# Product-key experts: four of eight token tiles gathered instead of two, keys swept in two passes and values in one

## The reference, cut to what matters

```python
q = (ht @ w_q).reshape(T, 8, 2, 128)
s = jnp.einsum('thpd,hpnd->thpn', q, sub_keys)          # 8 heads, 2 halves, 128 sub-keys
vals, idx = lax.top_k(s, 16)
cand = vals[:, :, 0, :, None] + vals[:, :, 1, None, :]   # 256 candidates a head
top_s, top_pos = lax.top_k(cand.reshape(T, 8, 256), 16)
experts = (i1 * 128 + i2)                                # 8 * 16 = 128 of 16384 experts a token
gates = jax.nn.softmax(top_s, axis=-1)
a = gelu(einsum('td,ted->te', xb, u_tab[eb]))            # key side
y = einsum('te,ted->td', gates * a, v_tab[eb])           # value side
x = x + gate2 * rmsnorm(y)
```

## Time and profile before

| | us |
|---|---|
| median of three runs | 3335.14 |
| lowest, highest | 3317.35, 3335.84 |
| profiled execution, first to last instruction | 3333.3 |
| PE, DVE, ACT, POOL busy | 3133.5, 2255.8, 1016.9, 1005.3 |
| first key product to last key product | 719.5 to 2218.6 |
| first value product to last value product | 2225.9 to 3307.5 |
| granted TensorE clock, mean | 0.976 |

### The profile page before, as it was taken

How to read it: one execution, slowest core, us unless ns; L and a number is a source line. 1 busy time by engine, 2 the same in 40 slices (tenths; PEclk the granted TensorE clock), 3 DMA queues, 4 the chain that set the end, 5 groups by cost and what they waited for, 6 DMA issues and landing times. The chain is left out here.

```text
span 3333.3 us, 44756 instructions
## 1 busy us (share of the span) xinstructions
PE 3133.5 (94%) x14706; PEld 2592.3 (78%) x14706; DVE 2255.8 (68%) x3986; ACT 1016.9 (31%) x1301; POOL 1005.3 (30%) x735
## 2 busy tenths in 40 slices
PE   3993799989999999999999999998999998999996
PEld 3881587878888888888888888876888886788885
DVE  6345643567767677675876754436888888888886
ACT  3123442112232232322222221122333334333333
POOL 0000100013222233232332310024555567765541
PEclk9995899999999999999999999999999999999998
DMA  6510122222333324333233332248999999999995
GB/s 235 189 50 8 49 105 93 84 72 113 126 148 139 148 88 151 141 149 137 101 142 145 150 137 106 102 159 299 373 353 361 364 357 332 369 357 364 348 361 186
DMA packets 251520, 640.90 MB, mean 192 GB/s; under 512 B 28864, under 2 KB 134464, under 8 KB 249792
## 3 DMA queue, kind: packets, MB, share of 16 engines
q1 hardware_dynamic: 204528, 498.87, 40.8%
q0 software_dynamic: 46928, 141.20, 11.3%
HBM read 505.76 MB, written 134.22 MB: 192 GB/s over the span
## 5 line engine op out<-in xcount | busy, mean ns | idle before, releaser
L1393 POOL TENSOR_TENSOR onehot<-onehot,slots 128x1024 fp32r<-128x1024 f32 x192 | 368.9, 1943 | 1180.1 <-DVE onehot L1479 1180.1
L93 PE MATMUL acc_u<-a_hi,u_hi 128*128 128x512 f32 x2048 | 633.1, 391 | 2.5 <-PEq L1114 2.5
L93 PE MATMUL acc_u<-a_lo,u_hi 128*128 128x512 f32 x2048 | 632.3, 390 | 0.0
L93 PE MATMUL acc_u<-a_hi,u_lo 128*128 128x512 f32 x2048 | 631.6, 389 | 0.0
L1882 PE MATMUL y_ps<-v_hi,c_hi 128*128 128x512 f32 x1536 | 477.2, 392 | 32.6 <-DVE c_lo L83 26.8
L1882 PE MATMUL y_ps<-v_lo,c_hi 128*128 128x512 f32 x1536 | 475.8, 391 | 0.0
L1882 PE MATMUL y_ps<-v_hi,c_lo 128*128 128x512 f32 x1536 | 474.6, 390 | 0.0
L78 ACT ACTIVATE v_hi<-v_raw 128x1024 fp32r<-128x1024 f32 x256 | 271.6, 1061 | 654.0 <-PE y_ps L1882 544.8
L93 PEld LDWEIGHTS acc_u<-a_lo,u_hi 128*128 128x128 f32 x2048 | 385.0, 188 | 81.0
L93 PEld LDWEIGHTS acc_u<-a_hi,u_lo 128*128 128x128 f32 x2048 | 384.8, 188 | 81.2
L83 DVE TENSOR_TENSOR v_lo<-v_raw,v_hi 128x1024 fp32r<-128x1024 f32 x256 | 316.6, 1237 | 186.4 <-ACT v_hi L78 145.1
(11 more groups left out here) (228 smaller groups left out, 3414.4 us busy)
## 6 DMA issues: line engine op xcount, KB each, us to landing
v_raw<-in_v SPq DMA_DIRECT2D x256, 512.0 KB
u_raw<-in_u SPq DMA_DIRECT2D x128, 512.0 KB, 4.3
act_d<-gelu SPq DMA_DIRECT2D x128, 512.0 KB, 2.6
gate_d<-gate_block SPq DMA_DIRECT2D x12, 4096.0 KB, 12.1
gt<-gate_d SPq DMA_DIRECT2D x64, 768.0 KB
at<-act_d SPq DMA_DIRECT2D x256, 192.0 KB
w_mod_b<-in_w_mod SPq DMA_DIRECT2D x6, 2560.0 KB, 9.1
w_mod<-in_w_mod SPq DMA_DIRECT2D x9, 1024.0 KB, 16.4
```

Of the source, the lines that this page charges most:

```text
L93: done = pe.matmul(acc[:, cols], w, a[:, k, cols], start=first, stop=last)
L1393: last_op = pool.tensor_tensor(onehot_2[u][:, :, part, :], onehot_2[u][:, :, 0, :].bitcast(F32), gate.unsqueeze(2).to_broadcast([P, TOK // ...
```

## The change

It touches everything after `mix_out`. One block `experts` takes the place of three; all loops are written out, and every engine's list runs over 384 steps m: 128 key blocks for the first three tiles (pass one), the same 128 key blocks for the other five (pass two), 128 value blocks for the last four tiles. The first four tiles are gathered. Three of them have their top-16 search in the retrieval stage, three tiles at a time; the other five have it in steps 5 to 204, two heads at a time. Gate tables of the four dense tiles are made in batches of 8 tokens, one batch in every third step from step 44. There GpSimd no longer computes: it only issues the 512 row and 512 activation fetches, which are consumed from step 134 on, two rows a step, three in steps 200 to 255. The candidate list of a head holds 136 sums instead of 256.

```diff
-SPARSE = 2
-DENSE = TT - SPARSE
+EARLY = 3
+GATHERED = 4
+LATE = TT - EARLY
+DENSE = TT - GATHERED
+HEAD_TILES = EARLY
+STAGES = 4
+RAWS, SPLITS, GELUS, ACTS, ROWS = 4, 3, 3, 4, 7
+TURN = 8
+STEP_STAGES = ((0, 1), (2,), (3,), (4, 5), (6, 7), (8, 9), (10,), (11,), (12,))
+TOPK_FROM, TOPK_PERIOD = 5, 40
+BATCH = 8
+GATE_BATCHES = P // BATCH
+GATE_STEPS = GATE_BATCHES + 1
+GATES_FROM, GATES_EVERY = 44, 3
+ROWS_FROM, ROWS_FAST = 134, 200
...
+def topk_stage(g, dve, stage, scores, tops_out, chosen_out, read_all, done):
...
+    dve.drain()
+    if stage == 0:
+        for c in cs:
+            for p in range(2):
+                dve.max(vals[:, c, p, 0:8], scores[c][p])
+    elif stage == 1:
+        for c in cs:
+            for p in range(2):
+                dve.max_index(idx[:, c, p, 1 - p:9 - p], vals[:, c, p, 0:8], scores[c][p])
+                last = dve.match_replace(rest[:, c, p, :], vals[:, c, p, 0:8], scores[c][p], LOWEST)
...
+def split_expert_hi(g, act, m):
+    act.wait_ge(g.raw_in[m % RAWS], 16 * (m // RAWS + 1))
+    if m >= SPLITS:
+        act.wait_ge(g.tile_done, m - SPLITS + 1)
+    split_hi(act, g.hi[m % SPLITS][:], g.raw[m % RAWS][:]).then_inc(g.hi_ready, 1)
...
+def expert_product(g, pe, m):
+    pe.wait_ge(g.lo_ready, m + 1)
...
+    if m < N:
+        parts = [(acc[:, 0:EARLY * P], slice(0, EARLY * P))]
+    else:
+        wide = LATE * P // 2
+        parts = [(acc[:, half * HALF:half * HALF + wide], slice(EARLY * P + half * wide, EARLY * P + (half + 1) * wide))
+                 for half in range(2)]
...
+def retrieval_scalar(g, act):
...
+    for n in range(QTILES):
+        act.wait_ge(g.q_done, n + 1)
+        act.activation(g.q[n % 2][:], g.mps[n % 2][:], ACT.Copy).then_inc(g.q_out, 1)
+        if n + 2 < QTILES:
...
+            split_hi(act, g.wq_hi[n % 2][:], g.wq_raw[n % 2][:]).then_inc(g.wq_hi_ready, 1)
...
+        if n:
+            stage_out(n - 1)
+def retrieval_vector(g, dve):
...
+    for h in range(HEADS - 1):
+        split(2 * h + 2)
+        dve.wait_ge(g.s_out, 2 * h + 2)
+        for stage in range(5):
+            head_stage(g, dve, h, stage)
+        split(2 * h + 3)
+        for stage in range(5, TOPK_STAGES):
...
+            head_stage(g, dve, h, stage)
+def retrieval_tensor(g, pe):
...
+    for n in range(2, QTILES):
+        score(n - 2)
+        product(n)
+    score(QTILES - 2)
+    expert_product(g, pe, 0)
+    score(QTILES - 1)
...
+def sweeps_scalar(g, act):
...
+    for m in range(3 * N):
+        if m >= 2 * N - 1 and m + 1 < 3 * N:
+            split_coefficients(m + 1 - 2 * N)
+        if m + 2 < 3 * N:
+            split_expert_hi(g, act, m + 2)
+        x, batch = gate_turn(m - 1)
+        if x is not None and batch >= 0:
+            gate_evacuation(x * GATE_BATCHES + batch)
...
+        if m < 2 * N:
+            activate(m)
...
+    def onehots(b, u):
...
+        for t in range(BATCH):
+            col = slice(first + t, first + t + 1)
+            dve.tensor_scalar(g.onehot_1[u][:, t, :], g.iota, g.slots[:, 0, col], None, ALU.is_equal)
+            last = dve.tensor_scalar(g.onehot_2[u][:, t, :], g.iota, g.slots[:, 1, col], g.slots[:, 2, col],
+                                     ALU.is_equal, ALU.mult)
+        last.then_inc(g.onehot_ready, 1)
...
+    for m in range(3 * N):
+        if 2 * N - 2 <= m < 3 * N - 2:
+            coefficients(m + 2 - 2 * N)
+        if m + 2 < 3 * N:
+            split_expert_lo(g, dve, m + 2)
...
+        topk_steps(m)
+        x, batch = gate_turn(m)
+        if x is not None and batch >= 0:
+            onehots(x * GATE_BATCHES + batch, m // N)
...
+        for e in range(rows_by(m - 1), rows_by(m)):
+            add_row(e)
...
+def sweeps_gpsimd(g, pool):
...
+    for turn in range(turns):
+        for e in range(turn * TURN, (turn + 1) * TURN):
+            fetch_row(e)
+            if e == turn * TURN and turn + 1 < turns:
+                pick_acts(turn + 1)
+def sweeps_tensor(g, pe):
...
+    def gates(b, u):
+        pe.wait_ge(g.onehot_ready, b + 1)
...
+        for t in range(BATCH):
+            last = pe.matmul(g.gps[:, t, 0:NKEYS], g.onehot_1[u][:, t, :], g.onehot_2[u][:, t, :], start=True, stop=True)
...
+    for m in range(2 * N):
+        if m:
+            expert_product(g, pe, m)
...
+            gates(x * GATE_BATCHES + batch, m // N)
+    for n in range(N):
+        dense_product(n)
```

More of the change, by code:

```diff
@@ new lines, in head_stage, with pair_stage @@
+def head_stage(g, dve, h, stage):
+    scores = [[g.stage[(2 * h + p) % STAGES][:, c, :] for p in range(2)] for c in range(HEAD_TILES)]
+    topk_stage(g, dve, stage, scores, g.tops_r[:, :, h, :], g.chosen_r[:, h].rearrange("p c k l -> p (c k l)"),
+               g.heads_read, g.heads_done)
+def pair_stage(g, dve, x, pair, stage):
+    work = g.s_work[(x * PAIRS_OF_HEADS + pair) % 2]
+    scores = [[work[:, c, p, :] for p in range(2)] for c in range(2)]
+    heads = slice(2 * pair, 2 * pair + 2)
+    topk_stage(g, dve, stage, scores, g.tops_a[:, x % 2, heads, :],
+               g.chosen_a[:, x % 2, heads].rearrange("p h k l -> p (h k l)"), g.pairs_read, g.pairs_done)
@@ L1040, in topk_head, with shift_topk, norm_topk @@
+def shift_topk(g, dve, gates, tops, n):
+    dve.drain()
+    dve.tensor_tensor(gates, tops, tops[:, :, 0:1].to_broadcast([P, n, TOPK]), ALU.subtract).then_inc(g.shifted, 1)
+def norm_topk(g, dve, gates, n, turn):
+    norm = g.norm[:, 0:n]
+    dve.wait_ge(g.exps, turn + 1)
+    dve.tensor_reduce(norm, gates, AX, ALU.add)
     dve.drain()
[L1041 to L1044 removed]
+    dve.reciprocal(norm, norm)
@@ new lines, in topk_turn, with gate_turn, gate_buffer, gate_stores @@
+def topk_turn(m):
+    x, at = divmod(m - TOPK_FROM, TOPK_PERIOD)
+    return (x, at) if m >= TOPK_FROM and x < TOPK_TILES else (None, None)
+def gate_turn(m):
+    step, odd = divmod(m - GATES_FROM, GATES_EVERY)
+    if m < GATES_FROM or odd or step >= DENSE * GATE_STEPS:
+        return None, None
+    x, at = divmod(step, GATE_STEPS)
+    return x, at - 1
+def gate_buffer(b):
+    block = b // 2
+    return block % 2 if block < EARLY_BLOCKS else 2
+def gate_stores(s, block):
+    return len([n for n in range(block) if gate_buffer(2 * n) == s])
@@ new lines, in retrieval_sync, with store @@
+def retrieval_sync(g, sp):
+    i = g.i
+    sp.dma_start(g.keys[:], i["keys"]).then_inc(g.keys_in, 16)
+    for m in range(RAWS):
+        load_raw(g, sp, m)
+    def store(n):
+        sp.wait_ge(g.s_out, n + 1)
+        pair, head, lane = n // 4, n // 2 % 2, n % 2
+        sp.dma_start(g.s_d[:, pair, :, head, lane, :].rearrange("t p m -> p t m"), g.stage[n % STAGES][:, HEAD_TILES:, :])\
+          .then_inc(g.s_stored[n % STAGES], 16)
+    for n in range(QTILES):
+        if n + 2 < QTILES:
+            sp.wait_ge(g.wq_lo_ready, n + 1)
+            sp.dma_start(g.wq_raw[n % 2][:], i["w_q"][n + 2]).then_inc(g.wq_in[n % 2], 16)
+        if n:
+            store(n - 1)
+    store(QTILES - 1)
@@ new lines, in retrieval_tensor, with product, score @@
+def retrieval_tensor(g, pe):
+    def product(n, halves=(0, 1)):
+        pe.wait_ge(g.wq_lo_ready, n + 1)
+        tile_product(pe, g.mps[n % 2], g.wq_hi[n % 2], g.wq_lo[n % 2], g.a_hi, g.a_lo, halves).then_inc(g.q_done, 1)
+    def score(n):
+        pe.wait_ge(g.q_out, n + 1)
+        if n >= 2:
+            pe.wait_ge(g.s_out, n - 1)
+        for t in range(TT):
+            last = pe.matmul(g.sps[n % 2][:, t, :], g.q[n % 2][:, t * P:(t + 1) * P], g.keys[:, n, :], start=True, stop=True)
+        last.then_inc(g.s_done, 1)
+    for n in range(2):
+        product(n, halves=(1,))
+    pe.wait_ge(g.keys_in, 16)
+    for n in range(2, QTILES):
[4 more added lines that the diff above has]
+    score(QTILES - 1)
@@ L1135, in _ @@
[L1135 to L1140 removed]
+            retrieval_sync(g, sp)
+            sweeps_sync(g, sp)
         @block.scalar
         def _(act):
[L1144 to L1146 removed]
@@ L1187, in _ @@
+            sweeps_vector(g, dve)
+        @block.gpsimd
+        def _(pool):
+            sweeps_gpsimd(g, pool)
         @block.tensor
         def _(pe):
-            def product(n, s, halves=(0, 1)):
-                pe.wait_ge(lo_ready, n + 1)
-                tile_product(pe, acc[s], w_hi[s], w_lo[s], g.a_hi, g.a_lo, halves).then_inc(q_done, 1)
-            def score(n, s):
-                pe.wait_ge(q_out, n + 1)
-                for t in range(TT):
-                    last = pe.matmul(sps[s][:, t, :], q[s][:, t * P:(t + 1) * P], keys[:, bass.ds(n, 1), :],
-                                     start=True, stop=True)
-                last.then_inc(s_done, 1)
```

1243 lines of the change are left out of this document (511 added, 732 removed).

## The result

The changed kernel takes **3611.0 us** (median of four runs, 3594.8 to 3622.3) against 3334.5 for the kernel before (3317.4 to 3335.8): a ratio of 1.083, 95% interval 1.079 to 1.087. The forecast was 3283 us, range 3200 to 3385: the sign was wrong, and the time lies 226 us above the range. The profiled execution took 3607.6 us, 327 more than the 3281 of the sum.

A forecast was written before the change was run, and what follows sets the result against it. The prediction took TensorE's matmuls to bound both sweeps, with little DMA room in the value sweep. Query products +101, passes one and two +180, value sweep -326 and end -7 gave -52: 3281 in the span, 3283 us forecast, range 3200 to 3385.

The forecast's parts named there:

- TensorE's own work: Matmul time on TensorE: value sweep -349, key sweep +31, gates +24, together -294 us; 384 columns cost 0.173 us, 320 cost 0.146.
- 896 + 68 + 1: Pass two: the forecast's 896 us of key products, 68 of gates and 1 more, without its waits or gather delay.
- query wait: Query products: product 2h+3 waits for five search stages put ahead of its low part; seven turns of 14.4 us, +101 us.
- Gate batches: Gate steps: TensorE waits for one-hots of the same step, 0.2 us each; +86 us in pass one, +22 in pass two.
- a rival of its own (0.13), rival 4: Gate waits: the clock falls in them, 2 us each for 30 batches, giving 3343 us; chance 0.13.
- Gathering, pass two: GpSimd's gather in pass two: 161 rows at 2.8 us, 451 us against 421, with seven rows buffered; +30 us.
- Two rows a step [...] free: Gather in pass two: two rows a step cost GpSimd 5.6 us against a 7.6 us step, so no delay.
- rival 2: Steps 200 to 361: GpSimd's gather decides; at 3.3 us a row +144 us, 3427 us in all; chance 0.18.
- Value sweep: Value sweep: DMA makes 106 steps take 6.0 us, 22 take 5.45; 756 us, +58 over the matmuls.
- GpSimd's 5.6 is covered by it: Value sweep: GpSimd's 5.6 us for two rows hides behind the 6.0 us DMA step, adding nothing.
- End: After the last matmul: no sparse tile is finished there, last store at 8.5 instead of 15.8 us, -7 us.

The follow-up runs named there:

- e2: Changed kernel with the low part of query tile 2h+3 put back ahead of the search; 3586.5 us, 1.072.
- e9: Changed kernel with GpSimd issuing one pick behind each row instead of eight picks in a row; 3457.0 us, 1.041.
- e1: Changed kernel without GpSimd's picks and row fetches, the sums reading a row already in SBUF; 3266.7 us, 0.977.
- e7: e3 without the 512 row fetches, picks still in groups of eight; 3094.2 us, 0.933.
- e18: e9 run again on another chip, beside a repeat of the changed kernel; 3560.5 us, 1.066.
- e6: e3 without the 512 picks, coefficients made from the gates alone, all rows still fetched; 3107.1 us, 0.937.
- e3: Changed kernel with VectorE making the one-hots of a gate step one step earlier; 3435.7 us, 1.027.
- e15: e3 with at most three rows in flight, picks still in groups of eight; 3744.6 us, 1.123.
- e13: e3 with TensorE's steps 147 to 194 written as a loop, the other steps left written out; 3410.4 us, 1.023.
- e11: e3 with one pick behind each row and the rows spread over pass two and the value sweep; 3153.6 us, 0.951.
- e16: e11 with the low part of query tile 2h+3 ahead of the search; 3252.0 us, 0.977.
- e4: Kernel before the change with TensorE's loop over the value sweep written out; 3342.0 us, 1.000.
- e12: e11 with TensorE's steps 147 to 194 and 198 to 245 written as two loops; 3155.8 us, 0.952.

## Why the prediction was wrong, step by step

**TensorE's own work** was right: 384-column matmuls stand 0.173 us apart, 320-column ones 0.147 (below), and without its waits pass two takes 971 us where the terms 896 + 68 + 1 make 965.

**The query wait** had the right size for a partly wrong reason, which is luck in part: 81.6 us of waits, last product at 813.3 for 814.5. I ascribed all to the order; e2 shows 26 us for it, and the rest stays when the order is put back.

**Gate batches.** 91.9 us in 26 waits for 86, one-hots 0.20 and 0.25 us apart (in order of time, VectorE):
```profile
1124.87 0.28 DVE L1558 TENSOR_SCALAR onehot<-consts,slots 128x128 f32<-128x128 f32 x1
1125.06 0.34 DVE L1559 TENSOR_SCALAR onehot<-consts,slots 128x128 f32<-128x128 f32 x1
1125.32 0.28 DVE L1558 TENSOR_SCALAR onehot<-consts,slots 128x128 f32<-128x128 f32 x1
```
The failed part is that I gave the clock a rival of its own (0.13) because one wait of 3.39 us had left it up. One wait is not 26 of them, twelve us of product apart. It cost 47 us. With 6 us of longer waits and 9 of rest this is the +62 of pass one.

**Gathering, pass two: the step that failed.** The prediction has "**+30**" from seven buffered rows and 2.8 us a row, and "Two rows a step [...] free". Without the gather pass two is 1005 (my terms: 987); with it 1214. Two causes of these 209 us can be named. First GpSimd's rate: in the last 300 us of pass two e9 fetched 98 rows, 3.06 us each. 161 rows at that rate less the 421 us of their steps are 72 us, and e9's pass two is 71 over e1's (two chips, neither run with gaps).

The reason that I gave for rival 2, VectorE's instructions beside GpSimd's, is in the trace. GpSimd and then VectorE in a stretch of the changed kernel's value sweep:
```profile
3006.60 1.54 POOL L1699 DMA_INDIRECT picked_act<-act_early,aidx  x1 [0.30 <-issue]
3008.45 1.70 POOL L1706 DMA_INDIRECT rows<-in_v,eidx  x1 [0.30 <-issue]
3010.45 0.94 POOL L1706 DMA_INDIRECT rows<-in_v,eidx  x1 [0.30 <-issue]
3011.70 0.94 POOL L1706 DMA_INDIRECT rows<-in_v,eidx  x1 [0.30 <-issue]
```
```profile
3006.10 1.23 DVE L97 TENSOR_TENSOR lo<-raw,hi 128x1024 fp32r<-128x1024 f32 x1 [0.62 <-issue]
3007.24 0.68 DVE L97 TENSOR_TENSOR free_hi_r<-cf,free_hi_r 128x512 fp32r<-128x512 f32 x1
...
3008.04 1.28 DVE L1613 SCALAR_TENSOR_TENSOR ys<-rows,coef,ys 128x1024 f32<-128x1024 f32 x1
3013.60 1.29 DVE L1613 SCALAR_TENSOR_TENSOR ys<-rows,coef,ys 128x1024 f32<-128x1024 f32 x1 [4.28 <-DMA rows<-in_v,eidx]
```
A fetch takes GpSimd 0.94 us while VectorE stands, and longer beside VectorE's instructions on two tensors. Of the 413 fetches from 2764 to 3459 us, the 95 that had no VectorE instruction in their first 0.94 us took 0.93 to 0.95 us, the 256 that had instructions on two tensors (row sums, low parts, coefficients) for 0.8 us of it took 1.55 in the mean. In pass two, 38 fetches beside one-hots and searches, on one tensor, took 0.96. In e7, which moves no rows, fetches take 0.95 and 1.48 in the same two cases, so it is not the row transfers. So instructions on two inputs do lengthen a fetch, as the reason said. Of the fast mode the trace has little but one-hots of 128 columns beside a fetch, so that half stays open; and VectorE was busy for 69% of the value sweep, not 90%. The other way round nothing shows: VectorE's row sums took as long beside the fetches as without any (e1, second row):
```profile
L1613 DVE SCALAR_TENSOR_TENSOR ys<-rows,coef,ys 128x1024 f32<-128x1024 f32 x504 | 627.3, 1281 | 174.1 <-DMA rows<-in_v,eidx 166.4
```
```profile
L1611 DVE SCALAR_TENSOR_TENSOR ys<-gate_rows,coef,ys 128x1024 f32<-128x1024 f32 x504 | 623.4, 1282 | 2.1
```

Second, the starving, which no rival had. One of its stretches in the changed kernel, TensorE in order of time:
```profile
2294.80 0.46 PE L1306 MATMUL mix<-a_hi,lo 128*128 128x320 f32 x2
2295.09 0.48 PE L1306 MATMUL mix<-a_hi,hi 128*128 128x320 f32 x2
2295.42 0.31 PE L1306 MATMUL mix<-a_lo,hi 128*128 128x320 f32 x1
2296.59 0.30 PE L1306 MATMUL mix<-a_lo,hi 128*128 128x320 f32 x1 [0.87 <-issue]
...
2300.14 0.31 PE L1306 MATMUL mix<-a_hi,hi 128*128 128x320 f32 x1 [1.82 <-issue]
2300.29 0.31 PE L1306 MATMUL mix<-a_lo,hi 128*128 128x320 f32 x1
2302.95 0.43 PE L1306 MATMUL mix<-a_lo,hi 128*128 128x320 f32 x1 [2.36 <-issue]
2303.18 0.74 PE L1306 MATMUL mix<-a_hi,lo 128*128 128x320 f32 x2
2303.71 0.74 PE L1306 MATMUL mix<-a_hi,hi 128*128 128x320 f32 x2
```
Up to 2295.4 a pair starts every 0.29 us; then single matmuls in the middle of a product start up to 2.7 us apart, with nothing to wait for, and the pairs behind them start 0.53 us apart, the lower clock level. 123 such gaps cost 128 us. That can't be added to the 72: in e18 against e9 the gaps cost 126 us and pass two grew by 114, while TensorE's waits for the next gate product shrank from 63.5 to 33.8 us beside them (both shown above). How the changed kernel's 209 us divide between the two is not shown. Nor is a gap a matter of full DMA engines. In the same stretch, while the first gaps opened, they were nearly idle:
```profile
2295.00:2298.00 3.00, 1.57 (x8) 1.02 (x7) 0.00 (x0) 0.00 (x0) 2.28 (x3) 1.00 0.03 4
```
Of the 123 gaps 25 fall where the DMA engines were under 10% busy, 76 where they were over 80%.

**Value sweep.** The step had the wrong resource: "I take 6.0" for the DMA, and "GpSimd's 5.6 is covered by it". DMA was not the limit (e6). GpSimd fetched 214 rows in 695 us, 3.25 us each, 6.5 a step. Its groups in that stretch:
```profile
L1706 POOL DMA_INDIRECT rows<-in_v,eidx x214 | 272.2, 1272 | 73.2 <-issue 64.6 <-DVE ys L1613 8.5
L1699 POOL DMA_INDIRECT picked_act<-act_late,aidx x128 | 185.3, 1448 | 39.0 <-issue 39.0
```
It waits 8.5 us for VectorE in all. In the earlier trace rows a pick took 1209 ns and a row 1084, with 147 us of waiting for VectorE. The 2.8 us of the prediction were read from a GpSimd that waited for a sum's end before half of its rows (56 of 113): from 2300 to 2760 us of the kernel before 6 of 224 fetches began beside a row sum, here 109 of 413. Before a row that waits for nothing GpSimd idles 0.30 us; the 0.157 of the prediction is a mean over all 113. 107 steps at 6.5 and 21 at 5.45 are 810 us; 22 of the 832 remain. Rival 2's rate (3.3 us, 3427 us, chance 0.18) was the right one here, and it was not priced with rival 4. The two together, 144 + 60 us over the forecast's side, would have come to about 3490. The starving was priced nowhere.

**End:** 11.8 us, 7 less than forecast.

**What stays open** is what the starving is. Shown: it needs GpSimd's fetches (e1 against e3, one chip); it appears beside the three kernels before with medians of 3335 to 3339 us and beside neither of 3317 to 3319, so it goes with the chip or with where its memory lies (the chip of the first result is not on record, and its four runs of the kernel before have one of 3317.4); it is heaviest where three rows a step are asked, and was least with three rows in flight (e15); loops do not remove it (e13), and it comes with the DMA engines full and idle. Neither picks alone nor rows alone were run on a chip that starves, so which of the two it takes isn't known. The changed kernel itself wasn't run on a chip without it; e9, which differs by the order of its picks, has 1.041 on one, so starving is not needed to make the change slower.

**The version that beats both** is e11: one-hots a step ahead, picks between rows, rows spread evenly: 0.951. Its like on a chip that starves (e16) has 0.977. The query wait of some 80 to 100 us is still in it.

## What to carry to other kernels

A queue engine that has slack at today's demand must be priced at the rate that it shows when it never waits, and beside what its neighbours will be doing then: here 0.94 us a fetch alone and 1.55 beside VectorE's instructions on two tensors. Its work should be spread over all the time there is: the same 600 fetches cost nothing at seven rows in three steps and 80 us at two and then three a step. Waits that come back every few products cost their own length and half as much again in clock (92 and 47 us). When two unrelated cures both remove all of a loss, run the uncured kernel beside them on the same chip before believing either.

## What the runs showed of the hardware

- Single matmuls can start 0.5 to 3.6 us apart, with no wait shown, while GpSimd's picks and row fetches run, on three of five chips (20 to 179 gaps in pass two); on the other two there were none beside the same fetches. Such gaps come where the DMA engines are 3% busy (2295 to 2298 us of the changed kernel) and in loops beside which no 16 KB packet of instructions moves (e13).
- GpSimd's indirect DMA of a pick or of a row took 0.94 us with VectorE idle, 1.55 in the mean beside VectorE's instructions on two tensors of 512 or 1024 columns, and 0.96 beside short ones on one tensor (one-hots, searches). VectorE's row sums took 1281 ns beside the fetches and 1282 without.
- 92 us of idle in 26 pieces of about 3.5 us held the granted clock at 0.89 over 520 us (1030 to 1550 us of the changed kernel); it is 1.00 without them (e3).
- A pick and a row together took GpSimd 2.8 us when it had slack, and 3.06 (e9, end of pass two) and 3.25 (changed kernel, value sweep) when it had none.
- Long written-out stretches of TensorE's list cost no time against loops (e4: the value sweep; e12: 96 steps of pass two).
